# Pairwise decay sums of the scan: fp32 products with eight moving triangles, or split fp32r products with the triangle as stationary side

## The reference, cut to what matters

```python
adt = (dt * a)...                       # one decay per row and head
a_cs = jnp.cumsum(adt, axis=-1)
seg = a_cs[..., :, None] - a_cs[..., None, :]
decay = jnp.exp(jnp.where(causal, seg, -jnp.inf))
y_diag = jnp.einsum("bcgls,bcgrls,bcsgrp->bclgrp", cb, decay, xdt)
```

## Time and profile before

| what | value |
|---|---|
| median of three executions | 2472.85 us |
| the profiled execution's own time | 2477.41 us |
| its span, first to last instruction | 2475.3 us |
| PE busy | 2404.4 us (97%) |
| DVE busy | 1298.8 us (52%) |
| ACT busy | 879.4 us (36%) |
| POOL busy | 374.9 us (15%) |

### The profile page before, as it was taken

How to read it: one execution, slowest core, us unless ns; L and a number is a source line. 1 busy time by engine, 2 the same in 40 slices (tenths; PEclk the granted TensorE clock), 3 DMA queues, 4 the chain that set the end, 5 groups by cost and what they waited for, 6 DMA issues and landing times.

```text
span 2475.3 us, 34710 instructions
## 1 busy us (share of the span) xinstructions
PE 2404.4 (97%) x14354; PEld 2009.5 (81%) x14354; DVE 1298.8 (52%) x2101; ACT 879.4 (36%) x1499; POOL 374.9 (15%) x301
## 2 busy tenths in 40 slices
PE   8999999999999999999999999999999999999999
PEld 6778888888887777656888887988989878877788
DVE  3775625543535776875333336366565445554433
ACT  4331211111224444444222224364545333444422
POOL 0210000000014444501000001143343410000000
PEclk9999999999999999999999999999999999999999
DMA  9834334434321111012333332221222121121222
GB/s 324 204 94 125 119 103 130 126 119 118 104 68 35 52 38 48 35 44 76 92 96 102 95 93 86 69 69 52 69 69 78 60 69 52 52 69 52 77 94 111
DMA packets 252744, 220.79 MB, mean 89 GB/s; under 512 B 7480, under 2 KB 243443, under 8 KB 252204
## 3 DMA queue, kind: packets, MB, share of 16 engines
q1 hardware_dynamic: 249072, 217.92, 28.7%
q10 hardware_dynamic: 3260, 0.58, 0.1%
q0 software_dynamic: 256, 0.07, 0.0%
HBM read 214.26 MB, written 6.29 MB: 89 GB/s over the span
## 4 chain that ended last, share of the span: by engine, by line
PE 59%; ACT 3%; DVE 3%; issue 2%; POOL 1%; DVEq 0%; ACTq 0%; POOLq 0%
PE two L685 10%; PE bank L1354 5%; PE bank L1545 4%; PE bank L685 4%; PE bank L1350 3%; PE bank L1331 3%; PE two L1285 3%; PE bank L1526 2%; PE bank L1051 2%; PE two L1156 2%; PE bank L1182 2%; PE two L1565 2%; PE bank L1021 1%; PE bank L1033 1%; PE two L1297 1%
## 5 line engine op out<-in xcount | busy, mean ns | idle before, releaser
L2568 DVE TENSOR_TENSOR wL<-ring,wH 128x512 fp32r<-128x512 f32 x224 | 182.5, 829 | 225.3 <-ACT wH L1840 225.1
L1831 ACT ACTIVATE wH<-ring 128x2048 fp32r<-128x2048 f32 (+1 forms) x80 | 149.1, 1864 | 272.4 <-PE bank L690 73.4
L2557 DVE TENSOR_TENSOR wL<-ring,wH 128x2048 fp32r<-128x2048 f32 (+1 forms) x80 | 180.4, 2255 | 82.2 <-ACT wH L1831 82.0
L685 PE MATMUL two<-h1H,wH 128*128 128x512 f32 x496 | 195.5, 394 | 0.0
L685 PE MATMUL two<-h1H,wL 128*128 128x512 f32 x496 | 193.4, 390 | 0.0
L685 PE MATMUL two<-h1L,wH 128*128 128x512 f32 x496 | 193.3, 390 | 0.0
L1840 ACT ACTIVATE wH<-ring 128x512 fp32r<-128x512 f32 x224 | 133.6, 623 | 58.8 <-PE bank L1331 21.1
L1909 ACT ACTIVATE gateS<-two 128x512 f32<-128x512 f32 x44 | 26.3, 598 | 332.2 <-PE bank L690 142.0
L2661 DVE SCALAR_TENSOR_TENSOR xT<-two,ada,xT 128x512 f32<-128x512 f32 (+1 forms) x48 | 30.6, 679 | 186.2 <-PE bank L690 66.3
L3204 POOL TENSOR_TENSOR rstd<-rstd,sq 128x768 f32<-128x768 f32 (+1 forms) x15 | 30.4, 2024 | 611.4 <-ACT sq L1867 610.2
L1354 PE MATMUL bank<-unH,wH 128*128 128x272 f32 (+1 forms) x368 | 112.2, 305 | 3.9 <-ACT cin L2100 2.1
(11 more groups left out here) (642 smaller groups left out, 6953.5 us busy)
## 6 DMA issues: line engine op xcount, KB each, us to landing
ring<-in_ffn_w_in SPq DMA_DIRECT2D x88, 512.0 KB, 5.1
ring<-in_w_in SPq DMA_DIRECT2D x40, 1024.0 KB, 5.0
ring<-in_w_ada SPq DMA_DIRECT2D x32, 1024.0 KB, 5.2
ring<-in_ffn_w_out SPq DMA_DIRECT2D x16, 1024.0 KB, 5.1
early<-in_w_ada SPq DMA_DIRECT2D x12, 1024.0 KB, 12.0
ring<-in_diff_w_in SPq DMA_DIRECT2D x12, 1024.0 KB, 5.2
ring<-in_w_proj_ssd SPq DMA_DIRECT2D x8, 1024.0 KB, 4.9
ring<-in_ffn_w_out SPq DMA_DIRECT2D x8, 768.0 KB, 4.5
```

The source lines that it names most:

```text
L685: m = nc.tensor.matmul(bank[3 * s + half], w, r[:, 0:LAT], start=i == 0, stop=i == n - 1)
L1831: nc.scalar.activation(hi, raw, ACT.Copy).then_inc(w_hi, 1)
L2557: nc.vector.tensor_tensor(lo, raw, hi.bitcast(F32), ALU.subtract).then_inc(w_lo, 1)
L2568: nc.vector.tensor_tensor(lo, raw, hi.bitcast(F32), ALU.subtract).then_inc(q_lo, 1)
```

## The change

- `segments(n)` swaps the sides: the stationary side is always the constant triangle `lower` (lowerR, in fp32r), and the moving side is `upper` times the decays, four heads (512 columns) at once. The decays are split into a high fp32r part and a low one (adtR), so there are 2 x 2 = 4 products of 512 columns instead of 8 fp32 products of 128; the second pair adds to the same banks and waits for its own POOL instruction.
- `decays(n)` on POOL writes the tile useg with two instructions of 128x1024 (high part, low part) instead of one.
- Once, at slot (-1, 23): ACT copies adt to adtR (128x160) ahead of its two exponentials, DVE subtracts to get the low part; DVE copies `lower` to lowerR behind line 2937. These wait for the copy of the block's input to memory (x_out), because the new tiles lie where it was read from.
- Tiles move: ckT and cqT become parts of one tile on partitions 0 and 32, the decay chain's temporaries lie in the region that is given back before the scan, ysq gets its own tile.

```diff
-        ckT, cqT = sb("ckT", [16, ALL]), sb("cqT", [16, LAT])
+        sumsT = sb("sumsT", [48, ALL])
+        ckT, cqT = sumsT[0:16, :], sumsT[32:48, 0:LAT]
+        lowerR = sb("lowerR", [P, P], F32R)
+        adtR = sb("adtR", [P, 2, 5, 32], F32R)
...
-        lseg = sb("lseg", [P, 8 * P])
+        useg = sb("useg", [P, 2, 8, P], F32R)
...
-                pe.wait_ge(p_lseg, n + 1)
+                pe.wait_ge(p_lseg, 2 * n + 1)
                 if n:
                     pe.wait_ge(e_exp, n)
                 else:
                     pe.wait_ge(d_cta, 1)
-                for h in range(8):
-                    m = nc.tensor.matmul(two[0][:, h * P:(h + 1) * P], lseg[:, h * P:(h + 1) * P], upper, start=True, stop=True)
+                for x in range(2):
+                    if x:
+                        pe.wait_ge(p_lseg, 2 * n + 2)
+                    for h in range(0, 8, 4):
+                        m = nc.tensor.matmul(two[0][:, h * P:(h + 4) * P], lowerR[:], useg[:, x, h:h + 4, :].rearrange("p h s -> p (h s)"),
+                                             start=x == 0, stop=x == 1)
                 m.then_inc(e_seg, 1)
...
                 if (g, t) == (-1, 23):
+                    act.wait_ge(d_adt, 1)
+                    act.wait_ge(x_out, 16)
+                    nc.scalar.activation(adtR[:, 0], adt[:], ACT.Copy).then_inc(d_adt, 1)
                     act.wait_ge(d_sums, 1)
...
+            dve.wait_ge(x_out, 16)
+            link(nc.vector.tensor_copy(lowerR[:], lower))
...
+                if (g, t) == (-1, 23):
+                    dve.wait_ge(d_adt, 2)
+                    link.wait()
+                    nc.vector.tensor_tensor(adtR[:, 1], adt[:], adtR[:, 0].bitcast(F32), ALU.subtract).then_inc(d_adt, 1)
...
                     else:
-                        pool.wait_ge(d_adt, 1)
-                    nc.gpsimd.tensor_tensor(lseg[:, 0:8 * P].rearrange("p (h s) -> p h s", h=8), wide(adt[:, i, hs], P, P),
-                                            lower.unsqueeze(1).broadcast_to([P, 8, P]), ALU.mult).then_inc(p_lseg, 1)
+                        pool.wait_ge(d_adt, 3)
+                    for x in range(2):
+                        nc.gpsimd.tensor_tensor(useg[:, x], wide(adtR[:, x, i, hs].bitcast(F32), P, P),
+                                                upper.unsqueeze(1).broadcast_to([P, 8, P]), ALU.mult).then_inc(p_lseg, 1)
```

More of the change, by code:

```diff
@@ L315, in bass_two_blocks_kernel @@
         yold, xds, zA, gab = gap[:, 0, :], gap[:, 1, :], gap, gap
-        ckT, cqT = sb("ckT", [16, ALL]), sb("cqT", [16, LAT])
+        sumsT = sb("sumsT", [48, ALL])
+        ckT, cqT = sumsT[0:16, :], sumsT[32:48, 0:LAT]
+        lowerR = sb("lowerR", [P, P], F32R)
+        adtR = sb("adtR", [P, 2, 5, 32], F32R)
+        xm = sb("xm", [P, 4, META])
         stt4 = sb("stt4", [P, 8])
@@ L320, in bass_two_blocks_kernel @@
         zrow = sb("zrow", [P, 4, 512])
[L321 to L325, removed]
+        ysq = sb("ysq", [P, 512])[:]
         phase()
@@ L331, in bass_two_blocks_kernel @@
         wd = (sb("wdH", [P, KC, 48], F32R), sb("wdL", [P, KC, 48], F32R))
+        early_x = sb("early_x", [P, 1768])
+        dtt = sb("dtt", [P, 4 * 240])
+        dta, dtu, dtw, dtl = (dtt[:, 240 * k:240 * k + 240].rearrange("p (a n) -> p a n", a=5) for k in range(4))
+        expa = sb("expa", [P, 32])
+        logf = sb("logf", [P, 5, 16])
+        dtr = sb("dtr", [P, 5, 48])
+        adt = sb("adt", [P, 5, 32])
         leave()
@@ L341, in bass_two_blocks_kernel @@
                 cacc = sb("cacc", [P, 2, ALL])
-        dtr = sb("dtr", [P, 5, 48])
         dtv = sb("dtv", [P, 5, 32])
-        adt = sb("adt", [P, 5, 32])
         dec = sb("dec", [P, 352])
         CBm = sb("CBm", [P, P])
-        xm = sb("xm", [P, 4, META])
         xdt = sb("xdt", [P, 2, 512])
-        lseg = sb("lseg", [P, 8 * P])
+        useg = sb("useg", [P, 2, 8, P], F32R)
         Mt = sb("Mt", [P, 8, P])
```

## The result

Over 20 executions each, the changed kernel took 2477.85 us (median, 2473.25 to 2481.15) and the kernel before 2473.97 (2471.32 to 2478.33): a ratio of 1.0013, 95% interval 1.0008 to 1.0019. In a later comparison the ratio was 1.0018 [1.0009, 1.0028]. In the medians the change costs 3.9 and 4.6 us. I had forecast 1.3 us of gain; the time is inside the range, but the sign is wrong and clear of noise.

What follows compares the result with a forecast made beforehand. PE, busy 97% of the span, was taken as the bound. Gains of 4.30, 1.24 and 0.1 less losses of 0.5, 1.9, 1.12 and 0.86 gave 1.26 us gained: 2471.6 us from 2472.85, range 2461 to 2478.5.

Steps and rivals of the forecast that it cites:

- PE's part: PE's segments products: 0.86 us saved per n, at most 13.8; +4.30 at the five n where PE bounds itself.
- POOL's part: Decays on POOL: 16 more instructions of 1.89 us, each able to hold a DVE instruction on SBUF inputs for 1.89.
- n = 1, 14: PE waits there for DVE's cacc or for POOL, so its saving is idle time: 0 gained.
- n = 15: POOL's second instruction queues behind a DVE split; PE's second pair ends about where the group ends now: +0.1 us.
- n = 2 and the hold of n = 3: PE's second pair waits for POOL at n = 2: -0.5 us; POOL's second of n = 3 holds DVE: -1.9.
- the prediction's last paragraph: Signs to look for, among them PE waiting some 1.5 us between its two pairs at n = 2.
- n = 5, 9: wL that PE stands for comes 0.86 us earlier but waits 0.24 for POOL; 0.62 kept, twice: +1.24.
- n = 7, 11: POOL's second instruction delays DVE 1.89 us against 1.33 of slack: -0.56 each, -1.12 together.
- n = 3, 7, 11 with POOL's second of n = 4, 8, 12: Group starts: wL races POOL's second instruction, -0.86 us if POOL is first, else +0.86; weighed two to one: -0.86 for three.
- the table's sum: Distances between first segments products, n = 0 to 15: forecast -1.16 us, measured +6.89.
- the third: Rival: DVE becomes the bound, each second instruction delays a wL with under 1.89 us slack: +8.6 us, 2481.4; chance 0.13.
- The sign that I had named: PE's waits for wL and cin should grow from some 6 us to about 15.

Runs made afterwards that it cites:

- e8: Changed kernel; only POOL's second instruction of n = 3, 7, 11 waits for the last low part of its weight block: 2475.40 us, ratio 1.0006.
- e1: Changed kernel with one POOL instruction per n; PE's second pair rereads the high part, so the low part is left out: 2462.70 us, ratio 0.9960.
- e4: Changed kernel with three fp32 products of 512 columns put on PE ahead of the wait at the starts of groups 1 to 3: 2475.45 us, ratio 1.0004.
- e9: Kernel before, with DVE writing the last low part at the starts of groups 1 to 3 three times over: 2482.91 us, ratio 1.0042.
- e10: The kernel of e9 with three fp32 products of 512 columns on PE ahead of the same wait: 2478.44 us, ratio 1.0020.
- e3: Changed kernel; POOL's second instruction of n = 3, 7, 11 and 4, 8, 12 waits for the weight block's last low part: 2468.94 us, ratio 0.9982.
- e11: Changed kernel with the low part's instruction on DVE instead of POOL, two slots ahead of PE's products: 2467.10 us, ratio 0.9975.
- e7: Changed kernel; only POOL's second instruction of n = 4, 8, 12 waits for the last low part of the weight block: 2470.21 us, ratio 0.9986.
- e2: Changed kernel with PE's eight fp32 products as before, low part left out, POOL's two instructions per n kept: 2484.71 us, ratio 1.0050.
- e5: The kernel of e3 with one fp32 product filling PE at the starts of groups 1 to 3, four for two in group 0's gap: 2469.68 us.
- e6: Kernel before with one fp32 product filling PE at the starts of groups 1 to 3, three for two in group 0's gap: 2472.62 us.

## Why the prediction was wrong

By its own steps:

1. *PE's part, 0.86 per n*: right, 0.88 on average over the five stretches where PE is its own bound (4.40 against 4.30).
2. *POOL's part*: right in kind and size. 32 instructions with a minimum of 1.89 us and a median of 2.34; fp32r output costs nothing more. DVE's instruction on SBUF inputs stands still until POOL's ends (wL 2.25, L2915 2.13). The Trainium skill adds ("SBUF — State Buffer", "Who interferes with whom") that the order of issue decides who blocks; here POOL's came first at all three group starts, by 0.2 us.
3. *n = 1, 14*: right, no gain: PE's waits there grew by the 0.86 (for CBm from 0.7 to 1.6, for POOL's gap from 0.4 to 1.3). At n = 15 some 0.3 was gained, forecast 0.1.
4. *n = 2 and the hold of n = 3*: 3.16 lost, forecast 2.40. The hold was 1.66 of it (e8; forecast 1.9), so n = 2 was the term that was too small: 1.5 instead of 0.5. PE waited 1.54 us there between its pairs, as the prediction's last paragraph had it.
5. *n = 5, 9*: 0.64 kept, forecast 1.24. I had taken a wL as what PE stands for; the trace has no such wait there. PE waited for acc, 0.6 us before and 1.4 after, and e1, without the second instruction, has the same stretches (52.75 us).
6. *n = 7, 11*: 0.97 lost, forecast 1.12; e8 gave both back.
7. **The step that failed: "n = 3, 7, 11 with POOL's second of n = 4, 8, 12".** I weighed the race two to one and put 0.86 us for all three. POOL won all three, which by the same sentence's price is 2.6 instead of 0.86; e4, with the clock held up, shows 2.03. The other 5.75 us had no term at all. By my own numbers the stall of 1.2 us grows to 2.9 (1.2 + 0.86 + 0.86); I read a granted clock of 1.00 around it in the profile before, and took it as given for a stall more than twice as long. e9 and e10 show that a stall of 2.6 us brings the clock down with POOL untouched, and that a fall costs 1.55 us.

Without the falls the table's sum is 6.89 - 5.75 = +1.1, where I had -1.2. Steps 4, 5 and the race of step 7 make 2.5 us of the difference, steps 1 and 6 give 0.25 back; the clock is the rest of the error. The nearest of the rivals was the third (each second instruction delays a wL), right in place and sign; its price of 1.89 us at ten sites was not what happened: three sites cost 7.78. The sign that I had named came too: PE's waits for wL and cin grew from 5.6 to 14.9 us, where I had said about 15.

That the time lies inside the range is luck. The scan alone, 6.89 us on the 2473.97 of the kernel before, would give 2480.9; the part outside the scan, which I hadn't looked at, brought it back.

What stays open: the scan takes 6.9 us more, whole runs only 3.9 and 4.6. In the other experiments the median moved against the kernel before as the scan did, within 1.6 us (e3: 4.7 less, the scan 5.1). In the profiles the difference lies in the stretch from 1525 to n = 0, 2.9 us shorter in both of the changed kernel because the clock did not fall there; profiles of variants of both kernels have it with and without a fall. Why the changed kernel's 20 runs lie so low as a whole wasn't settled.

## What to carry to other kernels

Work that is moved from a busy engine to an idle one is not free: ask whom the idle engine's instruction makes stand still, and whether that list is the one the busy engine waits for; here the same instruction on DVE (e11) or behind the critical split (e3) turned a loss of 0.13% into a gain of 0.25% or 0.18%. A stall of TensorE has a second price when it grows: look at the granted clock behind the longest stalls, not at its mean, which stayed 0.99. And price a race by its worst outcome if it recurs in every period, since all three fell the same way.

## What the runs showed of the hardware

- Stalls of TensorE at the group starts, amid dense work: of 1.2 us, never followed by a fall of the granted clock (kernel before, e1, e3, e7, e11: none in fifteen); of 1.9 us in two of three (e2); of 2.6 to 2.7 us in eleven of twelve (changed kernel twice, e8, e9). A fall lasted some 3 us at 1.2 GHz and cost 1.4 to 1.6 us, at one place about 7 us and 2.8.
- Products whose result nobody reads, put into the stall, kept the clock up (e4, e10: six of six). At stalls of 1.2 us they gained nothing (e5, e6).
- Leaving a group of fp32 products cost the next fp32r product 0.09 us; behind fp32r products of 512 columns that was gone.
- POOL's multiply of 128x1024 took 1.89 us at least, to fp32 and fp32r alike; DVE's 1.21.
- In the gap of group 0, where stalls of 1.6 and 0.6 us follow each other closely, the clock fell in the profiles of e1, e3, e4, e7, e8 and e11 and in neither of the changed kernel's; what decides there is open. It cost nothing over stretch 1-3.
